# Interleaving attention by head pairs with its own projections in a six-layer, one-core kernel

## What is computed

```python
h = rms_norm(x, norm_mix_g[2])
qkv = (h @ w_qkv).reshape(b, s, 3, 3, 16, 64)      # groups, (q, k, v), heads, width
for g, (window, dil) in enumerate(((128, 1), (512, 4), (2048, 16))):
    q = head_rms_norm(qkv[:, :, g, 0], q_gain[g])
    k = head_rms_norm(qkv[:, :, g, 1], k_gain[g])
    v = qkv[:, :, g, 2]
    o, lse = dilated_group_attention(q, k, v, bias_g, dil, (window // 2) // dil)
wts = softmax(stack(lses), axis=0)                   # over the three groups
x = x + einsum('gbsh,gbshe->bshe', wts, stack(outs)) @ w_o
```

## Time and profile before

| | us |
|---|---|
| median of 3 runs (2915.59 to 2919.42) | 2918.84 |
| the profiled execution | 2916.95 |
| its span in the trace | 2915.2 |
| PE busy, share of the span | 2592.3 (89%) |
| DVE busy | 1676.4 (58%) |
| ACT busy | 1193.9 (41%) |
| POOL busy | 533.6 (18%) |
| DMA queue of the weights, share of 16 engines' span | 35.9% |

### The profile page before, as it was taken

One profiled execution on the slowest core, in us unless ns is written; L12 is line 12 of the kernel. 1 busy time (PEld: TensorE's weight loads), 2 busy tenths in 40 slices (PEclk: granted clock), 3 DMA queues, 4 the chain that ended last, 5 costly groups with the idle time before them and its releaser, 6 DMA issues. The chain is left out here.

```text
span 2915.2 us, 49758 instructions
## 1 busy us (share of the span) xinstructions
PE 2592.3 (89%) x19384; PEld 2465.6 (85%) x19390; DVE 1676.4 (58%) x2753; ACT 1193.9 (41%) x1927; POOL 533.6 (18%) x410
## 2 busy tenths in 40 slices
PE   7999898997889888999899975789988999988998
PEld 6999787997788677999799974489987999988998
DVE  3778794666555444566466675346656454334665
ACT  2534563444444323444244452234444344334443
POOL 1110692000455000000000022000002555440000
PEclk9999799999899888999899986589998999988999
DMA  4465003454334521455155532034541212103452
GB/s 158 153 207 192 16 2 112 156 182 146 99 130 155 159 33 28 143 187 189 65 173 173 167 129 73 17 116 142 182 153 58 66 59 73 66 30 116 137 183 97
DMA packets 107152, 344.26 MB, mean 118 GB/s; under 512 B 20432, under 2 KB 26160, under 8 KB 106480
## 3 DMA queue, kind: packets, MB, share of 16 engines
q1 hardware_dynamic: 106992, 342.07, 35.9%
HBM read 340.86 MB, written 1.16 MB: 117 GB/s over the span
## 5 line engine op out<-in xcount | busy, mean ns | idle before, releaser
L134 PE MATMUL ps<-h_high,hi 128*128 128x256 f32 x2936 | 851.6, 290 | 53.9 <-DVE h_low L272 38.1
L135 PE MATMUL ps<-h_low,hi 128*128 128x256 f32 x2936 | 840.6, 286 | 0.0
L136 PE MATMUL ps<-h_high,lo 128*128 128x256 f32 x2936 | 840.1, 286 | 0.0
L101 ACT ACTIVATE hi<-raw 128x1024 fp32r<-128x1024 f32 x623 | 644.7, 1052 | 439.9 <-PE ps L136 426.0
L111 DVE TENSOR_TENSOR lo<-raw,hi 128x1024 fp32r<-128x1024 f32 x521 | 629.5, 1225 | 318.7 <-ACT hi L101 318.2
L134 PEld LDWEIGHTS ps<-h_high,hi 128*128 128x128 f32 x2936 | 573.0, 195 | 62.5 <-DVE h_low L272 41.6
L135 PEld LDWEIGHTS ps<-h_low,hi 128*128 128x128 f32 x2936 | 573.2, 195 | 0.4
L136 PEld LDWEIGHTS ps<-h_high,lo 128*128 128x128 f32 x2936 | 572.9, 195 | 0.0
L111 POOL TENSOR_TENSOR lo<-raw,hi 128x1024 fp32r<-128x1024 f32 x102 | 242.6, 2383 | 491.4 <-ACT hi L101 491.3
L134 PE MATMUL ps<-hidden_h,hi 128*128 128x256 f32 x1056 | 299.3, 283 | 10.0 <-DVE lo L111 9.6
L135 PE MATMUL ps<-hidden_l,hi 128*128 128x256 f32 x1056 | 298.0, 282 | 0.0
(11 more groups left out here) (429 smaller groups left out, 4410.7 us busy)
## 6 DMA issues: line engine op xcount, KB each, us to landing
raw<-in_weights SPq DMA_DIRECT2D x623, 512.0 KB, 3.4
at_bias<-bias_group SPq DMA_DIRECT2D x64, 64.0 KB, 2.6
s_bn<-in_s_bn SPq DMA_DIRECT2D x4, 512.0 KB, 4.9
consts<-in_consts SPq DMA_DIRECT2D x1, 1794.5 KB, 9.3
x<-in_x SPq DMA_DIRECT2D x1, 1024.0 KB, 5.0
s_cT<-in_s_b SPq DMA_DIRECT2D x1, 1024.0 KB, 7.3
s_cw<-in_s_c SPq DMA_DIRECT2D x1, 1024.0 KB, 10.9
s_cT<-s_rows SPq DMA_DIRECT2D x16, 64.0 KB, 2.7
```

The source lines that it names most:

```text
L101: act.activation(k.hi[:, item % CUT, :], k.raw[:, item % RAW, :], ACT.Copy).then_inc(k.item_rounded, 1)
L134: pe.matmul(out, wh, xh, start=start, stop=False, **more)
L135: pe.matmul(out, wh, xl, start=False, stop=False, **more)
L136: return pe.matmul(out, wl, xh, start=False, stop=stop, **more)
```

## The change

All the blocks from the norm to the output projection become one block, in one function `attention`. The norm is a `Prep` with the pending add, so products start on unscaled input; the token-wise factor `1/root` is applied where keys are read (`k.rs`), as a column to the values (`vcol`), and folded into the epsilon of the queries' norm (`qcol`). Weight items are reordered on the host (`qkv_items`): six of head pair 0 (three query, three key tiles), 24 of the values, six for each of pairs 1 to 7, then the output projection, now by input tile (`by_input`) so that an item can be used once one pair's output exists. `by_input` and `by_output` each give eight items.

The block then runs: pair 0's six projections, with the bias table and three root rows turned into columns; the values; **slots** 1 to 8. In slot `s` the pair `s - 1` attends (four steps) between the six projections of pair `s`; slot 8 has the output projection's items in their place. The last steps' `transposed` and `values` of a pair run at the start of the next slot. Queries are no longer scaled when read: their inverse norms become columns (`qi`, 12 per pair), used in `masked`, which now multiplies and adds. Query square sums are matmuls with two columns; key square sums are as before. `ACTIVATE` of `Sqrt` is now once a pair (`roots`) and `Exp` four times a pair, and the compiled program has an ACT_TABLE_LOAD ahead of each change from one to the other. POOL cuts all 80 items. The bias strips of a pair are fetched between the loads of the items. The output of a pair is split into its pair of parts straight from PSUM (`high`, `low`), with no `linear` and no `Parts` behind it.

```diff
-        sort_tokens(k, (ph, pl), falling=True)
-        project_heads(k, [(ph, pl)] * GROUPS, VEC_AT["attn_q_gain"], qT, scaled=True)
-        sort_tokens(k, (ph, pl), falling=False)
-        project_heads(k, srcs, VEC_AT["attn_k_gain"], kT, scaled=False)
-        token_major(k, [(srcs[g], v[:, g, :, :]) for g in range(GROUPS)])
-        attend(k, tab0, tab12, qT, kT, v, oT)
-        linear(k, k.hp, KT, KT, dve_out=residual(k), parts=(Parts(k, oT, k.hp, KT),))
...
+        def _(sp):
...
+            loads(k, sp, first + V_AT, GROUPS * KT)
+            sp.wait_ge(k.bias_written.s, b_w + 32)
+            sp.wait_ge(a.fill, 1)
+            bias(0)
+            bias(1)
+            for s in range(1, HP):
+                loads(k, sp, first + item(PER * s), PER)
+                if s + 1 < HP:
+                    bias(s + 1)
+            loads(k, sp, first + O_AT, HP)
...
+            def project(o):
+                if o >= 2:
+                    pe.wait_ge(a.read, o - 1)
...
+            def sums(o):
+                n, i = o // PER, o % PER
+                pe.wait_ge(a.sq, o + 1)
+                if i == 0:
+                    pe.wait_ge(a.kn, n)
+                if i < GROUPS:
+                    for b in range(2):
+                        mm = pe.matmul(query_sums(i, b), sq[:, o % 3, b * P:(b + 1) * P], two_heads[:, 0:P:64], start=True, stop=True)
+                else:
+                    mm = pe.matmul(key_sums(i - GROUPS), two_heads, sq[:, o % 3, :], start=True, stop=True)
...
+            for s in range(1, HP + 1):
+                q = 4 * (s - 1)
+                beside(s, 0)
+                if s > 1:
+                    values(q - 2)
+                    transposed(q - 1)
+                beside(s, 1)
+                if s > 1:
+                    values(q - 1)
+                beside(s, 2)
...
+                scores(q)
...
+                beside(s, 3)
+                transposed(q)
+                scores(q + 1)
...
+                beside(s, 4)
+                values(q)
+                transposed(q + 1)
+                scores(q + 2)
...
+                beside(s, 5)
+                values(q + 1)
+                transposed(q + 2)
+                scores(q + 3)
+                if s < HP:
+                    for i in range(3, PER):
+                        sums(PER * s + i)
...
+            def roots(n):
+                act.wait_ge(a.sum, PER * (n + 1))
...
+                act.activation(rt[:, 0:2 * T], k.ps[:, SUM, :], ACT.Sqrt, scale=1.0 / 64, bias=k.eps[:, 0:1])
+                act.activation(rt[:, 2 * T:3 * T], k.ps[:, SUM + 1, 0:T], ACT.Sqrt, scale=1.0 / 64, bias=k.eps[:, 0:1])
...
+            def normed(n, part):
+                if part == 0:
+                    dve.wait_ge(a.rt, n + 1)
...
+                    dve.reciprocal(qi[:, n % 2, :], rq[:, :])
+                    inverted(dve.reciprocal(k.ps[:, SUM, :], rt[:, 0:2 * T]))
+                    key(n, 0)
+                    key(n, 1)
+                else:
+                    inverted(dve.reciprocal(key_sums(2), rt[:, 2 * T:3 * T]))
+                    key(n, 2).then_inc(a.kn, 1)
...
+                dve.scalar_tensor_tensor(sc[:, q % 2, 0:T], k.ps[:, S0 + q % 2, 0:T], qi[:, n % 2, c:c + 1], bias0[:, n % 2, hh, b, :], ALU.mult, ALU.add)
...
-            make_parts(k, norm(k, k.x, KT, VEC_AT["norm_mix_g"] + KT * layer, k.h, D, pair=k.hp, pending=True))
             attention(k)
```

More of the change, by code:

```diff
@@ L1349, in advance @@
[L1349 to L1363 removed]
+        ph, pl = sb("at_ph", [P, KT, T], F32R), sb("at_pl", [P, KT, T], F32R)
@@ new lines, in attention, with item @@
+        a.ol = k.sem("at_output_low_part")
+        a.wo = k.sem("at_output_projected")
+        a.fill = k.at_fill.s
+        a.bias = [b.s for b in k.at_bias]
+        steps = [(h, b) for h in range(AH) for b in range(2)]
+        b_in, b_p, b_t, b_w = k.side_here.n, k.bias_ps.n, k.bias_tab.n, k.bias_written.n
+        prep = Prep(k, VEC_AT["norm_mix_g"] + 2 * KT, Prep.RESIDUAL)
+        block = ctx.enter_context(nc.Block())
+        def item(o):
+            return o if o < PER else SLOTS_AT + o - PER
@@ new lines, in beside @@
+            def beside(s, i):
+                if s < HP:
+                    project(PER * s + i)
+                elif i < 4:
+                    for j in (2 * (i % 2), 2 * (i % 2) + 1):
+                        project_out(j, 4 * (i // 2), 4 * (i // 2) + 4)
+                else:
+                    project_out(i, 0, KT)
+            prep.sums_before(pe)
+            for j in range(KT):
+                prep.here(pe, j)
+                for o in range(2):
+                    mm = product(pe, projection(o), w.tile(o * ITEM + j), pair_tile(k.hp, j), start=(j == 0), stop=(j == KT - 1))
+                    if j == KT - 1:
+                        mm.then_inc(k.item_used, 1)
@@ new lines, in _ @@
+            for s in range(1, HP + 1):
+                q = 4 * (s - 1)
+                if s > 1:
+                    diagonal(q - 1)
+                beside(s, 0)
+                if s > 1:
+                    normed(s - 1, 0)
+                beside(s, 1)
+                if s > 1:
+                    normed(s - 1, 1)
+                    low(s - 2)
+                beside(s, 2)
+                masked(q)
+                diagonal(q)
+                masked(q + 1)
+                beside(s, 3)
+                diagonal(q + 1)
+                masked(q + 2)
+                beside(s, 4)
+                diagonal(q + 2)
+                masked(q + 3)
+                beside(s, 5)
@@ new lines, in _ @@
+            diagonal(4 * HP - 1)
+            low(HP - 1)
+            for n in range(KT):
+                if n == KT - 2:
+                    dve.wait_ge(k.item_used, first + O_AT + HP)
+                elif n % 2 == 0:
+                    dve.wait_ge(a.wo, n + 2)
+                dve.tensor_tensor(k.x[:, n, :], k.x[:, n, :], output(n), ALU.add)
+        k.side_here.n += 48
+        k.bias_ps.n += 1
+        k.bias_tab.n += 1
+        k.bias_written.n += 32
+        advance([k.at_sc, k.at_max, k.at_neg, k.at_exp, k.at_rd, k.at_diag, k.at_tr, k.at_cp, k.at_pv], len(steps))
@@ L1564, in last_norm @@
+        k.used += O_AT + HP
 def last_norm(k, post_col, out):
@@ L2016 @@
 GC = 64
-ACC_BANKS = 2, 3
 LEVELS = 6
```

603 lines of the change are left out of this document (364 added, 239 removed).

## The result

The changed kernel takes 2874.09 us (median) against 2919.13 us for the kernel before in the same measurement. The ratio of the two is 0.9847, with a 95% interval of 0.9829 to 0.9865. It is faster by 1.5%, where 2.5% was predicted; the median lies 0.09 us above the predicted range. One of its four executions took 3734.75 us at a mean granted clock of 0.63 and counts in the median but not in the ratio; the median of the other three, 2868.79 to 2874.86, is 2873.31. So the 0.09 us mean nothing by themselves, and the misses are better read stage by stage. The profiled execution took 2873.31 us, its span is 2871.5.

A forecast was written before the change was run, and what follows sets the result against it. TensorE was taken as the limit in values and projections, but standing at handovers and slowed by clock falls in attention. Start, values, slots, end and clock summed to 401.4 us against 473.65, giving 2847 us, range 2828 to 2874.

The forecast's parts named there:

- Start: From the first add to the values: six projections with sums, bias table matmuls and root columns, 30.8 us together.
- Values: The 24 value items at 2.79 us each, 67.0 us, at full clock, POOL's cuts costing nothing.
- Slots, work: TensorE's work in the slots: 42 projections with sums, eight output items and 32 attention steps, 263.5 us.
- (a): Chain from scores to `transposed`: hidden behind a projection and sum, except 0.2 us in each slot's first step, 1.4 us.
- (b): Keys before a slot's first scores: 8.2 us of DVE work hidden behind 9.3 of TensorE's, by 1.1.
- (c): End of a slot: TensorE waits 2.35 us for the last key's square behind the last `exp`, seven slots, 16.5 us.
- (d): First pair's bias strips, fetched behind the values' loads, hold TensorE for 2.9 us.
- (e): Last pair, with no projection to hide `copied`, `high` and `low`: a wait of 2.1 us.
- Clock: Granted clock falls behind five in seven of nine TensorE waits, 2.0 us each: 12.9 us, bounds 0 and 36.
- Longer chains: Rival: POOL's cuts beside attention slow VectorE's mask reduction and diagonal, lengthening (a) and (c): 2864 us; chance 0.23.
- The clock holds: Rival: no clock falls behind the slots' waits, 13 us less: 2834 us; chance 0.17.
- The clock stays low: Rival: TensorE stays at 1.2 GHz through the slots, their work taking twice as long: 3074 us; chance 0.03.

The follow-up runs named there:

- `best`: Changed kernel with last square earlier, strips early, one-word tile back, root-column passes behind the third projection, last-slot output tiles waiting for fewer keys: 2839.4 us, ratio 0.9724.
- the kernel with both edits: Changed kernel with each pair's last key read and squared earlier, and the first two pairs' bias strips fetched earlier: 2847.08 us, ratio 0.975.
- the kernel with early strips: Changed kernel with the first two pairs' bias strips fetched after eight of the values' weight items, not all 24: 2866.0 us, ratio 0.9824.
- the kernels with the square first: Changed kernel with each pair's last key read before the fourth step's mask and squared before its exp: alone 2856.15 us, ratio 0.9793; others add edits.

## Why the prediction was right and where it was wrong

**The bound and the plan of the sum held; one step of it failed, and several terms were mis-sized.** Taking each part of the stretch:

| part | predicted | measured |
|---|---|---|
| start | 30.8 | 34.5 |
| values | 67.0 | 67.0 |
| slots | 299.3 | 307.5 |
| of these work, waits, clock | 263.5, 22.9, 12.9 | 274.1, 20.1, 13.3 |
| end | 4.3 | 4.3 |
| stretch | 401.4 | 413.2 |
| outside | 0 | +16.7 |

**Start, +3.7.** Two projections (8.8 predicted, 8.88 measured) and their sums (3.6, 3.55) were right. The bias matmuls took 2.74 for 2.65 and the wait behind them 0.4 for 1, but the twelve tiny passes, given 0.7 with a bound of 2, took 2.57. They did so at the low clock, which had fallen behind the bias matmuls and that wait:

```profile
732.15:734.72 2.57, 2.57 (x13) 2.56 (x13) 2.57 (x4) 2.26 (x4) 0.82 (x1) 0.52 0.00 0
```

At full clock, in the kernel `best`, they take 1.42. The clock stayed down for the projection behind them (0.55 in the row above), and the last four projections with their sums took 16.3 us for 14.0. I had counted falls only in the slots; of the 3.7 us some 3.4 are this one fall.

**Values, right.** At 2.79 us an item and full clock, with POOL's cuts hidden, as said.

**Slots, work, +10.6: the mis-sized terms are the sums.** For the query's I took 0.24 us where "four short passes lie between 0.1 and 0.5". In the timeline of the changed kernel the next product starts 0.47 behind it:

```profile
923.22 0.61 PE L1415 MATMUL ps<-consts,at_squares 128*128 128x2 f32 x4
923.69 0.36 PE L134 MATMUL ps<-h_high,hi 128*128 128x256 f32 x1
```

That is 21 x 0.23 = 4.8 us, at the upper end of the bound given; doubling it added at least 0.33 each. So a pass with two moving columns costs some 0.12 us, as much as one with 256 in a product; its stationary side is a 128 by 128 tile of squares, and the four weight loads of a sum took 0.52 us at 873.55. The key's sum, for which the row of the kernel before gave 0.24, stands three in a row at the end of a slot. In the kernel with both edits, where no wait lies ahead of them, the three take 1.21 us for 0.72:

```profile
850.23 1.56 PE L1418 MATMUL ps<-at_squares,consts 128*128 128x256 f32 x6
851.44 0.47 PE L134 MATMUL ps<-h_high,hi 128*128 128x256 f32 x1
```

In seven slots that is 3.4 us. The other 2.4 lie in small amounts where one kind of matmul follows another: a projection that has small matmuls ahead of it took 3.05 to 3.15 for 3.04. Steps held, at 3.18 for 3.17.

**Slots, waits.** (a) was 0, not 1.4: the chain of a slot's first step (scores at 872.48, `transposed` at 877.11) just fits behind its projection and sum. The rule of the Trainium skill, "ScalarE: Activation LUTs", section "What ACT_TABLE_LOAD costs", which would have made this chain 1.4 us longer, is not borne out:

```profile
874.43 1.28 ACT L1602 ACT_TABLE_LOAD   x1
...
875.72 0.72 ACT L1602 ACTIVATE at_work<-at_work,at_stats 128x512 f32<-128x512 f32 x1
```

`exp` starts 0.01 us behind the load's end, and the load 0.02 behind the end of the rounding (873.37 + 1.04), so that between the three no drain of 1.38 us has room. (b) was hidden, as said, with so little to spare that it shows (0.16 us) once (c) is gone. (c) came seven times, at 1.91 and not 2.35 by the view of waits; from the scores' end to the last sum it is 929.91 to 932.95, 3.04 us for 2.9, but the two sums ahead cover 1.13 of it and not 0.55. (d) was 4.22 for 2.9. (e), the last pair, 0.5 + 0.7 + 1.4 = 2.6 for 2.1.

**Clock, right in the sum, and by luck in part.** The clock fell behind six of the seven waits (c), at 1.50 us each, the difference of two slots with and without a fall. The first slot is 9.97 longer than in the kernel with early strips: 4.22 of wait, 1.50 for the fall behind its (c), and 4.25 for the one behind (d). That makes 6 x 1.5 + 4.25 = 13.25 us for 12.9. But the forecast had 6.4 falls at 2.0 each: too much for those behind (c), too little for the one behind (d), and the two errors cancel.

**Outside, wrong: this is the step that failed.** It is in the prediction's first paragraph: "nothing outside it changes its work, so the whole sum is made there". The only reason given for putting the term outside at nothing is that the work there is the same. It is, but for one memset; its time changed by 16.7 us all the same, more than the 11.8 inside. The full diff showed the dropped tile. I had read it as clean-up. In its place the runs showed that dropping this one word costs the kernel before 15 us and the changed one about 8. Of the 16.7 us, 2.3 come with the slower transfers, which hang on the word; 3.4 with a return of TensorE's clock one step later in the S5 layer, which kernels with the word have too; and the rest in small amounts, most of them behind the stretch. What sets the time of that return, and what makes up the part behind the stretch, is open.

**The rivals.** "Longer chains" named the right region (2858 to 2874) for a wrong reason: the row maximum takes 0.686 to 0.689 us, those wholly beside a POOL cut included, for 0.686 before; the first mask 0.483 to 0.485 with a multiply, beside a cut or not, for 0.419 without. The diagonal takes 0.286, with one of 32 at 0.685, for 0.287. With that the Trainium skill, "GPSIMD Engine Reference", section "Key points", agrees, as far as the masks go. "The clock holds" is what the kernels with the square first show, for another reason: they have no wait behind which it could fall. "The clock stays low" did not come near.

## What to carry to other kernels

Ask, when a chain is hidden behind work of the bound engine, what stands at the end of the group, where no such work is left: here one square behind one `exp` cost 1.9 us seven times and a clock fall six times, and moving that square, and the read ahead of it, gave back 17 us. A wait of 1.9 us on TensorE cost 3.4 here where the clock fell behind it and 1.9 where it did not, and an edit can change which of the two it is, so compare stretches with the same granted clock before pricing an edit. And when a change drops or adds a tile, compare the untouched parts first, by a marker at their start and end, before the difference of the totals is ascribed to the edit. Where they differ, compare one engine's instructions one by one: the places where the difference grows are few.

## What the hardware showed that was not expected

- A tile of one word placed ahead of others moves them from a multiple of 64 bytes to 32 beyond one, and 16 transfers of 64 KB, by the median of the view that holds them, then land in 4.4 to 4.7 us, not in 2.7 to 3.0; the cut behind them comes 2.1 to 2.4 us later.
- The kernel before lost 15 us by it. In the changed kernel and its variants TensorE's clock came back to 2.4 GHz one or two steps later in the S5 layer, or one step earlier, at 3.4 us a step, by edits that do not touch that layer.
- After equal waits of 1.91 us, TensorE's clock fell behind six of seven in the changed kernel, behind every other one when three sums a slot were doubled, and in none of the slots between the first and the last where no wait was longer than 0.3 us.
- Twelve passes of one column each took 2.57 us of TensorE at a granted clock of 0.52, and 1.42 at 1.00. In the first case the clock had fallen behind a wait of 0.4 us, and was 0.55 for 4.9 us more; in the second it had fallen behind one of 0.7 us and was back by then.
